# Differential attention: the scores of both kinds of head formed in one place, the plain heads in swapped order

## The reference

```python
def attend(q, k, v):                      # differential attention, head size 32, two components c
    s = jnp.einsum('bqhcd,bkhcd->bhcqk', q, k, preferred_element_type=F32) * (A_QK ** -0.5)
    p = jax.nn.softmax(s, axis=-1)
    a = p[:, :, 0] - lam * p[:, :, 1]
    return jnp.einsum('bhqk,bkhd->bqhd', a.astype(v.dtype), v)
```

## Time and profile before

| what | value |
|---|---|
| median of 3 runs | 2429.42 us |
| profiled execution | 2430.29 us, span 2428.4 us |
| PE busy | 2296.2 us (95%), 10070 matmul instructions |
| DVE, ACT, POOL busy | 950.8, 529.4, 187.9 us |
| mean granted TensorE clock | 0.970 of full speed |
| stretch of the 16 steps | about 257 to 429 us |

### The profile page before, as it was taken

How to read it: one execution, slowest core, us unless ns; L and a number is a source line. 1 busy time by engine, 2 the same in 40 slices (tenths; PEclk the granted TensorE clock), 3 DMA queues, 4 the chain that set the end, 5 groups by cost and what they waited for, 6 DMA issues and landing times.

```text
span 2428.4 us, 28708 instructions
## 1 busy us (share of the span) xinstructions
PE 2296.2 (95%) x10070; PEld 1621.4 (67%) x10071; DVE 950.8 (39%) x1775; ACT 529.4 (22%) x1101; POOL 187.9 (8%) x181
## 2 busy tenths in 40 slices
PE   8999999867799898999999999999999999999999
PEld 2554566422333377678888888566676788888888
DVE  5532566430000135725335432444244434335421
ACT  3200465411111144522111100131231212111100
POOL 0000435011111100000000002202010000000000
PEclk9999999878899999989999999999999999999999
DMA  9221152659786931012222221312112122222230
GB/s 345 85 98 33 48 203 107 240 187 378 271 341 244 354 124 53 27 53 78 87 85 81 77 97 59 131 43 86 61 59 79 35 104 79 87 88 87 77 120 19
DMA packets 81023, 298.02 MB, mean 123 GB/s; under 512 B 8990, under 2 KB 8990, under 8 KB 80431
## 3 DMA queue, kind: packets, MB, share of 16 engines
q1 hardware_dynamic: 75102, 271.26, 31.6%
q0 software_dynamic: 5840, 25.67, 2.9%
HBM read 282.73 MB, written 14.16 MB: 122 GB/s over the span
## 4 chain that ended last, share of the span: by engine, by line
PE 87%; DVE 4%; ACT 2%; issue 2%; SPq 2%; DMA 2%; DVEq 0%; POOL 0%; ACTq 0%; POOLq 0%
PE products L1606 41%; PE products L992 8%; PE products L1436 6%; PE products L1216 6%; PE products L1511 3%; PE products L1454 3%; PE products L1770 2%; PE products L1267 2%; PE products L1688 2%; PE products L1345 1%; PE products L1561 1%; PE products L1280 1%; PE products L1235 1%; PE products L1256 1%; DMA weights_and_work<-in_experts 1%
## 5 line engine op out<-in xcount | busy, mean ns | idle before, releaser
L1606 PE MATMUL products<-normed,weights_and_work 128*128 128x264 f32 (+1 forms) x1520 | 348.7, 384 | 0.0
L1606 PEld LDWEIGHTS products<-normed,weights_and_work 128*128 128x128 f32 x1520 | 288.1, 190 | 50.7 <-issue 5.3
L1436 PE MATMUL products<-weights_and_work 128*64 128x512 f32 x768 | 181.3, 633 | 48.8 <-DMA weights_and_work<-in_experts 48.1
L1861 ACT ACTIVATE weights_and_work<-products 128x256 f32<-128x256 f32 (+3 forms) x221 | 95.6, 452 | 407.4 <-PE products L1606 156.4
L1606 PE MATMUL products<-weights_and_work,mixed 128*128 128x256 f32 (+1 forms) x800 | 182.3, 382 | 0.8 <-ACT weights_and_work L1861 0.8
L1436 PEld LDWEIGHTS products<-weights_and_work 128*64 128x64 f32 x768 | 65.6, 146 | 162.9 <-issue 161.2
L1606 PEld LDWEIGHTS products<-weights_and_work,mixed 128*128 128x128 f32 x800 | 151.8, 190 | 24.4 <-ACT weights_and_work L1861 1.6
L1606 PE MATMUL products<-weights_and_work 128*128 128x256 f32 (+1 forms) x672 | 151.0, 385 | 7.2 <-DVE residual L3238 5.2
L1606 PE MATMUL products<-weights_and_work,normed 128*128 128x264 f32 (+1 forms) x704 | 155.6, 382 | 0.0
L1606 PE MATMUL products<-normed,mixed 128*128 128x264 f32 (+1 forms) x672 | 154.1, 382 | 0.0
L1606 PEld LDWEIGHTS products<-weights_and_work 128*128 128x128 f32 x672 | 128.8, 192 | 28.1 <-issue 7.3
(11 more groups left out here) (562 smaller groups left out, 2959.4 us busy)
## 6 DMA issues: line engine op xcount, KB each, us to landing
weights_and_work<-in_weights SPq DMA_DIRECT2D x301, 512.0 KB, 4.3
weights_and_work<-in_experts SPq DMA_DIRECT2D x192, 512.0 KB, 5.4
results<-normed SPq DMA_DIRECT2D x8, 512.0 KB, 7.1
residual<-in_x POOLq DMA_DIRECT2D x1, 2048.0 KB, 15.3
weights_and_work<-in_dft_half POOLq DMA_DIRECT2D x1, 2048.0 KB, 14.1
token_rows<-mixed SPq DMA_DIRECT2D x4, 512.0 KB, 3.1
normed<-results SPq DMA_DIRECT2D x4, 512.0 KB, 6.8
mixed<-results SPq DMA_DIRECT2D x4, 512.0 KB, 7.3
```

Source lines behind the costliest of these rows:

```text
L1436: m = pe.matmul(ps[UNIT * b:UNIT * (b + 1), side, :], job_t[:, k, UNIT * b:UNIT * (b + 1)], expert_w[b][:, s, at:at + 512], start=(k == 0) ...
L1606: m = pe.matmul(bank(p, n), left(k), right(k), start=(fresh and k == 0), stop=(k == kt - 1), skip_group_check=True)
L1861: act.activation(out, src, ACT.Copy, scale=scale).then_inc(bank_free[p.bank], 1)
```

## The change

`scores(s, "A")` and `scores(s, "B")` become one `scores(s)`, called where A's was, with six matmuls in the order A, B, A, A, B, A. B's rows are now `DH - o` and on, which is the other half of the array from A's, so step `s` handles plain head `h ^ 1` instead of `h`; bias, values and place of the output follow. Both products' banks are waited for ahead of the first matmul. The wait on `half_scored` stands before the last matmul (second component, first 256 keys). Everything else of the order on PE, and all of that on ACT and DVE, is as it was.

```diff
--- before.py
+++ after.py
@@ -217,9 +217,10 @@
         r[name] = b.many(n)
 
 
-    def scores(s, kind):
+    def scores(s):
         if s < len(STEPS):
-            r["scores", s, kind] = b.take(0, 1, 2) if kind == "A" else b.take(3, 4)
+            r["scores", s, "B"] = b.take(3, 4)
+            r["scores", s, "A"] = b.take(0, 1, 2)
 
     def turned(s, kind):
         r["T", s, kind] = [b.take(5), b.take(6)]
@@ -228,13 +229,11 @@
         if s >= 0:
             r["PV", s, kind] = b.take(6)
 
-    scores(0, "A")
-    scores(0, "B")
+    scores(0)
     for s in range(len(STEPS)):
-        scores(s + 1, "A")
+        scores(s + 1)
         turned(s, "A")
         weighed(s - 1, "B")
-        scores(s + 1, "B")
         turned(s, "B")
         if s % 2 == 1:
             r["out_1", s // 2] = b.take(7)
@@ -1219,30 +1218,34 @@
                 finish(p, m)
 
             def attentions():
-                def scores(s, kind):
+                def scores(s):
                     if s == len(STEPS):
                         return
                     t, h = STEPS[s]
-                    p = r["scores", s, kind]
+                    a, b_ = r["scores", s, "A"], r["scores", s, "B"]
                     o = 64 * (h % 2)
-                    fill(p)
-                    if kind == "A":
-
-                        for c, at, key, width in ((0, 0, 0, 512), (1, NKEY, 0, 256), (1, 1024, 256, 512), (0, 512, 512, 256)):
-                            rows_ = slice(o + 32 * c, o + 32 * c + 32)
-                            if at == 512:
-                                pe.wait_ge(half_scored, s + 1)
-                            m = pe.matmul(wide(p, 2 * NKEY)[:, at:at + width], aq[rows_, h // 2, t * P:(t + 1) * P],
-                                          ak[rows_, h // 2, key:key + width], start=True, stop=True)
-                            if s == 0 and at == 0:
-                                begin(m)
-                            if at == NKEY:
-                                m.then_inc(half_scored, 1)
-                    else:
-                        for at, width in ((0, 512), (512, 256)):
-                            m = pe.matmul(wide(p, NKEY)[:, at:at + width], bq[o:o + DH, h // 2, t * P:(t + 1) * P],
-                                          bk[o:o + DH, h // 2, at:at + width], start=True, stop=True)
-                    finish(p, m)
+                    fill(b_)
+                    fill(a)
+
+                    def first(c, at, key, width):
+                        rows_ = slice(o + 32 * c, o + 32 * c + 32)
+                        return pe.matmul(wide(a, 2 * NKEY)[:, at:at + width], aq[rows_, h // 2, t * P:(t + 1) * P],
+                                         ak[rows_, h // 2, key:key + width], start=True, stop=True)
+
+                    def second(at, width):
+                        rows_ = slice(DH - o, 2 * DH - o)
+                        return pe.matmul(wide(b_, NKEY)[:, at:at + width], bq[rows_, h // 2, t * P:(t + 1) * P],
+                                         bk[rows_, h // 2, at:at + width], start=True, stop=True)
+
+                    m = first(0, 0, 0, 512)
+                    if s == 0:
+                        begin(m)
+                    second(0, 512)
+                    first(1, 1024, 256, 512)
+                    first(0, 512, 512, 256).then_inc(half_scored, 1)
+                    finish(b_, second(512, 256))
+                    pe.wait_ge(half_scored, s + 1)
+                    finish(a, first(1, NKEY, 0, 256))
 
                 def turn(s, kind):
                     of = prob_a[:, 0] if kind == "A" else prob_b
@@ -1259,12 +1262,13 @@
                 def weigh(s, kind):
                     t, h = STEPS[s]
                     a = "AB".index(kind)
+                    head = h ^ a
                     p = r["PV", s, kind]
                     fill(p)
                     for kt in range(NKT):
                         if kt % 4 == 0:
                             read(pe, r["T", s, kind][kt // 4])
-                        m = pe.matmul(ps[:, p.bank, 0:DH], prob_t[:, a, kt, :], vals[:, kt, a, h * DH:(h + 1) * DH],
+                        m = pe.matmul(ps[:, p.bank, 0:DH], prob_t[:, a, kt, :], vals[:, kt, a, head * DH:(head + 1) * DH],
                                       start=(kt == 0), stop=(kt == NKT - 1))
                     finish(p, m)
 
@@ -1971,8 +1973,9 @@
                     t, h = STEPS[s]
                     if kind == "B":
                         act.wait_ge(inv_b, s + 1)
+                    head = h ^ "AB".index(kind)
                     p = r["PV", s, kind]
-                    copy(p, o_tok[:, t % 2, "AB".index(kind), h * DH:(h + 1) * DH], bank(p, DH),
+                    copy(p, o_tok[:, t % 2, "AB".index(kind), head * DH:(head + 1) * DH], bank(p, DH),
                          row_inv[:, s % 2, 0:1] if kind == "A" else row_inv[:, s % 2, 2:3])
 
                 def roots(t):
@@ -2524,7 +2527,7 @@
                                           negate=True).then_inc(max_a, 1)
                     else:
                         sc = wide(p, NKEY)
-                        b = bias[:, h, 7 - 2 * t:15 - 2 * t, :].rearrange("p a b -> p (a b)")
+                        b = bias[:, h ^ 1, 7 - 2 * t:15 - 2 * t, :].rearrange("p a b -> p (a b)")
                         link(tt_(sc[:, C:NKEY], sc[:, C:NKEY], b, ALU.add))
                         dve.tensor_reduce(neg_max[:, s % 2, 2:3], sc, AX_X, ALU.max, negate=True).then_inc(max_b, 1)
```

## The result

| | before | changed |
|---|---|---|
| median of 4 runs | 2429.13 us (2425.87 to 2431.74) | 2485.74 us (2474.99 to 2489.31) |
| ratio | | 1.0226, 95% 1.0192 to 1.026 |
| profiled execution | 2430.29 us, span 2428.4 | 2489.31 us, span 2487.5 |
| mean granted clock, span | 0.970 | 0.949 |

Slower, as forecast, but by 57 us and not by 25, and outside the range of 2421 to 2464. All of it arises in the attention: from the first scores to the first load of the product behind the steps the stage takes 234.0 us instead of 173.4, 60.6 more, and the span is longer by 59.1.

What follows compares the result with a forecast made beforehand. TensorE (PE) was taken to bound the kernel, with 87% of the span. Quiet steps 17.4, steps 5, 9, 13 0.9 and the start 7 sum to 25 us, on 2429.4 giving 2454; range 2421 to 2464.

Steps and rivals of the forecast that it cites:

- The scores at 4.44: Six score matmuls per step: changed row counts empty the array, five pieces take 4.44 us, 1.13 more than 3.31.
- side by side: Rival on the score set: disjoint row groups run together whatever their count, set 2.25 us, kernel 2424; chance 0.26.
- The new wait at bank 6, +0.45 a step: Second turn of each quiet step: PE waits for ACT's copy to free bank 6, net +0.45 us.
- Steps 5, 9, 13: Attention steps where ACT has the roots: 0 in 5 and 13, at most +0.9 us in 9.
- The start: Scores of step 1 wait for both exponentials of step 0; PE idles, then works at half clock: +7 us.
- 11 x (1.13 + 0.45): Eleven quiet steps (1 to 4, 6 to 8, 10 to 12, 14), longer scores plus bank 6 wait: 17.4 us.
- the two ends of the set's length: Score set per step: 4.44 us if row-count changes empty the array, 2.25 if three row groups run side by side.
- bank 3: Rival: next step's scores wait for the plain head's exponential, margin 0.65 us; with side-by-side scores 2433; chance 0.07.

Runs made afterwards that it cites:

- e3_b32: Changed kernel with the plain head's scores formed over only 32 of their 64 rows, so all six matmuls have 32 rows: 2433.12 us, ratio 1.0003.
- e5_overlap: Changed kernel with plain heads not swapped, so the plain head's 64 rows contain the pair's: 2483.65 us, ratio 1.0221.
- e2_grouped: Changed kernel with the plain head's two matmuls first, then the pair's four in their old order: 2444.47 us, ratio 1.0065.
- e6_full: Changed kernel with one added, overwritten matmul of 128 rows by 512 columns within each set of scores: 2476.83 us, ratio 1.0204.
- e9_quarters: Changed kernel with the plain head's 64 rows as two adding groups of 32, short matmuls first, pair reported first: 2422.59 us, ratio 0.9955.

## Why the prediction was wrong in size

*The scores at 4.44: right.* Measured 4.42 in five pieces, with the sizes forecast. The reason was right too: e3_b32 takes 2.24 with the same order and equal counts, and e5_overlap shows that the place of the rows does not enter. The rival "side by side" fell at the first set. The rule of the Trainium skill (TensorEngine Tiling (Array Packing), Tiling Modes, Key Properties), that a change of mode drains TensorE, agrees: 4.42 with unequal counts, 2.24 with equal ones. What the Trainium skill says of loads in different row groups (TensorE: Matmul & The Clock Gate, Part 3, The mechanism), that they overlap running matmuls, this case shows only among equal counts: loads within 0.02 us in e3_b32, and 1.05 or 0.63 apart in the changed kernel.

*The new wait at bank 6, +0.45 a step: right at full clock.* PE idles 0.42 in e3_b32, e2_grouped and e6_full, and the step of e2_grouped is 0.35 longer for it. In the changed kernel the full-clock step is +1.44 where 1.13 + 0.45 = 1.58 was said. At half clock PE arrives later and the wait is all but gone (0.02 in the step of 312.35): it is paid only in the steps that are not slowed anyway.

*Steps 5, 9, 13: +0.9 forecast, +8.6 measured.* At full clock they were nearly right: in e6_full step 5 takes 13.09 us with its added matmul, no more than before's 13.27, since the scores there lie beside the normalisation; step 9 takes 13.56 against 11.27, of which up to 1.06 is the added matmul. Step 13 does not bear on it: it takes 18.45 there, at half clock in part, behind a wait of PE of 2.23 us for the plain head's exponential. In the changed kernel these steps run at half clock in part, 17.5, 14.5 and 14.5 us.

*The start: +7 forecast, +9.5 measured.* The mechanism is the one described: idle 6.08 (5.9 forecast), then half clock. Two terms are mis-sized, both by the clock. The first set was priced at full clock, 4.44, and took 5.9, as the clock fell within it. For the set behind the idle time I took 7.2, on the ground that the clock would be back within it as it was before; it took 277.50 - 269.24 = 8.3, all of it at half clock. What follows to step 2 took 6.1 where 6.3 was said.

*The step that failed: all quiet steps were priced at full clock.* "11 x (1.13 + 0.45)" takes the durations of a stretch whose mean granted clock was 0.97, and moves instructions in it as if the clock were a property of the stretch. It went with the order: before, 1.8 us of narrow scores stood between full-width work, then 1.5 us of them again; after, 4.4 us stand in one row, in which 32 or 64 rows of 128 are at work. PE is busy throughout, so nothing in the busy shares warns. The forecast looked at the clock in one place, behind the idle time of the start, and did not ask what else could lower it. e6_full, with quiet steps of 10.95 + 1.06 at 0.99, shows that this is the missing part. Its size is an estimate from the profiled execution: 60.6 less some 27 for the start and for the rest at full clock (9.5 + 14.4 + 1.2 and about 2 for steps 5 and 9), so 33 us.

*The range.* It was built from the two ends of the set's length and of the bank wait, and had no case in which the same instructions run slower. The rival "bank 3" was real but small: in steps with DVE held up the scores wait for the plain head's exponential, 7.1 us over the whole stage by the groups by line, of which 6.08 are the start.

What stays open: what it is in the changed kernel's set that lowers the clock, since 3.3 us of narrow scores in one row do not in e2_grouped; why the clock stayed up in one stretch of the changed kernel (414 to 426 us) with the same set in it, and why e3_b32 and e9_quarters, with sets of 2.25 us, still lose some (0.92 and 0.94). In both of them half clock begins at or just behind a wait of PE (1.50, 1.25 and 3.67 us in e3_b32, 1.92 in e9_quarters), but no run varies that alone.

## What to carry to other kernels

Before putting matmuls of different row counts beside each other, on whatever rows, cut them to one count: the same six matmuls took 4.42 us mixed and 2.24 with 32 rows each, and splitting the 64-row sum into two 32-row groups that add up in the bank costs nothing beside them. Moving narrow matmuls together can cost the granted clock as well as the time of the array: here it went from 0.97 to 0.76 over the stage with PE busier than before. So read the granted clock beside the busy share after such a move, and where it falls expect the neighbours to run slower too (here the turn 1.47 instead of 0.81, the product 1.60 instead of 0.86). And when one step reports two results, report first the one whose consumers run the longest chain: with the pair reported first the chain in e9_quarters no longer left PE for the wait at bank 6, and its quiet step is 8.41 against 8.79 in e3_b32, with sets of 2.26 and 2.24.

## What the runs showed of the hardware that was not expected

- The granted clock fell from 2.4 to 1.2 GHz within a set of 4.4 us of narrow matmuls while PE was 95% busy, in most steps, and one full-width matmul of 1.06 us in the middle of it kept it at 0.99. The same columns over 64 rows did not (0.77), nor did a full-width one behind the set (0.81). In e2_grouped a set of 3.3 us of narrow matmuls left it at 0.99.
- More work made a stretch faster: quiet steps of 12.01 us instead of 13.64.
- Matmuls of equal row count on different row groups start side by side, but their ends are reported in the order of issue: putting a 256-column matmul ahead of a 512-column one on the other group took 0.33 us from a set (1.82 to 1.49).
